# Wider contractions, joined scores and column halves in the attention stages of a three-block fp32 kernel

## The reference

```
# first block: 16 meta tokens are put ahead of the 512; queries see keys up to their own position
h = concatenate([meta, x])
y_sb = stick_breaking(q_sb, k_sb, v_sb)              # 4 heads of 64
y_sp = indexed_sparse_attention(...)                 # 4 heads of 64, top-k keys, softmax
p = softmax(q1 k1 + bias) - lam * softmax(q2 k2 + bias);  y_df = p @ v   # 4 heads, values 128 wide
# second block, nsa part: 6 query heads, 2 groups of keys, 3 kinds of keys, gated and added
kc = gelu(blk @ w1[0]) @ w2[0]; vc = gelu(blk @ w1[1]) @ w2[1]   # 31 compressed keys, blk 2048 wide, w1 2048x256
o = g0 * softmax(q kc) vc + g1 * softmax(q ks) vs + g2 * softmax(q kw) vw
# second block, rwkv part: 4 heads, a state of 64x64 each, carried over 512 tokens
state = state * w_t + sa * (kk_t * a_t) + v_t * k_t;  out_t = state @ r_t
# second block, moba part: 6 heads, causal softmax attention
```

## Time and profile before

| | |
|---|---|
| median of 3 runs | 2671.15 us |
| the profiled execution, its own time | 2670.03 us |
| its span | 2668.2 us |
| TensorE busy | 2564.4 us, 96% |
| VectorE, ScalarE, GpSimd busy | 56%, 39%, 11% |
| granted TensorE clock, mean | 0.985 |

### The profile page before, as it was taken

The page is one execution under the profiler, slowest core; times in us unless marked ns, Lnnn a source line. Parts: engine busy times, 40 slices in busy tenths (PEclk is TensorE's granted clock), DMA queues, the critical chain, the costliest instruction groups (busy, mean ns, idle before and its releaser), DMA issues.

```text
span 2668.2 us, 36243 instructions
## 1 busy us (share of the span) xinstructions
PE 2564.4 (96%) x14684; PEld 2083.5 (78%) x14684; DVE 1481.2 (56%) x2439; ACT 1028.3 (39%) x1817; POOL 300.0 (11%) x213
## 2 busy tenths in 40 slices
PE   8899999999999999999989999999999999999998
PEld 6688898999998877866567777878866687788886
DVE  4887644554445457476546877454744634433544
ACT  4465454443223253235543223254333333322323
POOL 0053210012222010000012222020000000000001
PEclk9999999999999999999999999999999999999999
DMA  4211122222323341520025664332221123233332
GB/s 170 84 53 56 50 63 64 72 87 88 95 89 94 95 143 48 173 72 2 1 95 169 196 203 142 95 103 88 87 71 56 56 87 95 79 95 95 95 95 71
DMA packets 76979, 244.81 MB, mean 92 GB/s; under 512 B 12708, under 2 KB 18213, under 8 KB 76558
## 3 DMA queue, kind: packets, MB, share of 16 engines
q1 hardware_dynamic: 69470, 215.72, 26.3%
q10 hardware_dynamic: 7344, 26.77, 3.0%
HBM read 238.25 MB, written 6.90 MB: 92 GB/s over the span
## 4 chain that ended last, share of the span: by engine, by line
PE 65%; DVE 10%; ACT 4%; issue 2%; POOL 0%; DMA 0%; SPq 0%; ACTq 0%; DVEq 0%
PE ps L595 54%; DVE wl L379 2%; PE ps L2766 2%; ACT wh L367 1%; DVE arena L1064 1%; PE ps L3453 1%; PE ps L1795 1%; PE ps L1824 1%; DVE xl L676 1%; PE ps L1813 1%; DVE arena L3123 1%; PE ps L769 1%; PE ps L3437 1%; PE ps L1660 1%; PE ps L1545 0%
## 5 line engine op out<-in xcount | busy, mean ns | idle before, releaser
L595 PE MATMUL ps<-xh,wh 128*128 128x512 f32 (+1 forms) x2728 | 1007.3, 384 | 22.7 <-DVE xl L676 7.4
L595 PE MATMUL ps<-xl,wh 128*128 128x512 f32 (+1 forms) x2728 | 989.3, 377 | 0.0
L595 PE MATMUL ps<-xh,wl 128*128 128x512 f32 (+1 forms) x2728 | 985.2, 376 | 0.0
L379 DVE TENSOR_TENSOR wl<-ring,wh 128x1024 fp32r<-128x1024 f32 x374 | 472.3, 1263 | 595.4 <-ACT wh L367 594.6
L367 ACT ACTIVATE wh<-ring 128x1024 fp32r<-128x1024 f32 x372 | 393.1, 1057 | 943.0 <-PE ps L595 841.4
L595 PEld LDWEIGHTS ps<-xh,wh 128*128 128x128 f32 x2728 | 500.9, 189 | 149.6 <-issue 40.6
L595 PEld LDWEIGHTS ps<-xh,wl 128*128 128x128 f32 x2728 | 500.4, 189 | 98.0
L595 PEld LDWEIGHTS ps<-xl,wh 128*128 128x128 f32 x2728 | 499.1, 189 | 97.3 <-issue 5.5
L2046 PE MATMUL ps<-xh,wh 128*128 128x264 f32 (+1 forms) x816 | 254.5, 312 | 5.3 <-DVE xl L433 3.8
L759 POOL TENSOR_TENSOR arena<-arena 128x512 f32<-128x512 f32 (+1 forms) x35 | 60.2, 1725 | 1637.0 <-ACT arena L744 1637.0
L2046 PE MATMUL ps<-xl,wh 128*128 128x264 f32 (+1 forms) x816 | 233.4, 286 | 0.0
(11 more groups left out here) (387 smaller groups left out, 2583.2 us busy)
## 6 DMA issues: line engine op xcount, KB each, us to landing
ring<-in_weights SPq DMA_DIRECT2D x374, 512.0 KB, 3.6
arena<-in_w_ada ACTq DMA_DIRECT2D x48, 512.0 KB, 4.6
arena<-in_cmp_w SPq DMA_DIRECT2D x2, 2048.0 KB
strip_copies<-strip_scratch SPq DMA_DIRECT2D x8, 327.5 KB, 7.0
arena<-strip_copies SPq DMA_DIRECT2D x8, 264.0 KB, 4.1
out_features<-arena SPq DMA_DIRECT2D x8, 256.0 KB, 2.1
token_scratch<-arena SPq DMA_DIRECT2D x3, 512.0 KB, 6.7
arena<-token_scratch SPq DMA_DIRECT2D x12, 128.0 KB, 4.3
```

The source lines that it names most:

```text
L379: dve.tensor_tensor(flat(self.wl[:, s % 2]), flat(self.ring[:, s % RING]), flat(self.wh[:, s % 2]).bitcast(F32), ALU.subtract).then_inc(se ...
L595: last = pe.matmul(self.place(u, e), w[:, k, :], x[:, k, o:o + m], start=(k == 0 and i == 0), stop=(k == self.chunks - 1 and i == 2))
```

## The change

Six edits; none changes which engine does what, and no DMA is added, removed or moved.

1. `PairAttention`: in steps with more than the meta keys, the transposes of the first 32 keys and the copy take all 128, and line 2603 contracts over all 128 rows of `VM` and `PM` (for the 4-query tile too).
2. `PairCausal`: the compressed shares are transposed, copied and contracted 128 wide in place of 31; the columns beyond the 31 meet rows of `VC` that a new memset has set to zero.
3. `PairCausal`: for the tiles i = 0 and i = 1 the scores of ks and kw come from one matmul of twice as many columns, in the step e = 0; the step e = 1 issues no scores.
4. `RwkvScan`: value part and U part come ahead of the state's part.
5. `Compress`: each first-layer matmul becomes two, on 64 output partitions each.
6. `Compress`, VectorE: the memset of `VC`.

```diff
@@ RwkvScan.tensor
-        def output(c):
-            k = c // 2
+        def within(c, F, f):
+            for h, lo, t in heads:
+                rows = pair_rows(c, h)
+                pe.matmul(out(c, lo, t), F[rows, t], chunks[rows, c // 2, t, f], start=(f == 3 and t == 0), stop=False)
+
+        def across(c):
             for t in range(2):
                 for lo in (0, 64):
-                    pe.matmul(out(c, lo, t), STATE[lo:lo + 64, c % 2, t], AR[lo:lo + 64, t, 1, c], start=(t == 0), stop=False)
-            for stop, F, f in ((False, V[:, k], 3), (True, U, 1)):
-                for h, lo, t in heads:
-                    rows = pair_rows(c, h)
-                    last = pe.matmul(out(c, lo, t), F[rows, t], chunks[rows, k, t, f], start=False, stop=stop and t == 1)
+                    last = pe.matmul(out(c, lo, t), STATE[lo:lo + 64, c % 2, t], AR[lo:lo + 64, t, 1, c], start=False, stop=t == 1)
...
-            output(c)
+            within(c, V[:, k], 3)
+            within(c, U, 1)
+            across(c)
@@ Compress
+        yield 16.9
+        self.core.vec.do(dve, dve.memset(self.VC.rearrange("p a b -> p (a b)"), 0.0))
...
-                    last = pe.matmul(self.place(2 * e + c), self.w1[:, l, c * P:(c + 1) * P], self.X[:, l], start=(l == 0), stop=(l == 15))
+                    for lo in (0, 64):
+                        last = pe.matmul(self.place(2 * e + c)[lo:lo + 64], self.w1[:, l, c * P + lo:c * P + lo + 64], self.X[:, l],
+                                         start=(l == 0), stop=(l == 15))
@@ PairCausal.tensor
         def score(s, x):
+            if x.first:
+                return
...
-                last = pe.matmul(ps[:, m, 0:(x.i + 1) * P], x.q[half, x.i * P:(x.i + 1) * P], x.keys[m][half, 0:(x.i + 1) * P],
-                                 start=True, stop=True)
+                keys, out = x.keys[m][half, 0:nk] if not x.joined else x.keys[m][half, :, 0:nk], ps[:, m, 0:nk]
+                if x.joined:
+                    out = ps[:, m, 0:2 * nk].rearrange("p (e n) -> p e n", e=2)
+                last = pe.matmul(out, x.q[half, x.i * P:(x.i + 1) * P], keys, start=True, stop=True)
...
-                    pe.transpose(ps[0:NCMP, self.bank(s), (e + 1) * P:(e + 2) * P], x.cmp[0][e], ident)
+                    pe.transpose(ps[:, self.bank(s), (e + 1) * P:(e + 2) * P], x.cmp[0][e], ident)
...
-                    last = pe.matmul(out[m], x.cmp[1][m], self.PM[0:NCMP, m * P:(m + 1) * P], start=False, stop=False)
+                    last = pe.matmul(out[m], x.cmp[1][m], self.PM[:, m * P:(m + 1) * P], start=False, stop=False)
@@ PairCausal.vector
-                    dve.wait_ge(self.scores.sem, self.scores.at(s + 1))
+                    dve.wait_ge(self.scores.sem, self.scores.at(sum(not a.first for a in self.steps[:s + 1])))
...
-                dve.tensor_tensor_reduce(out=self.X[:, s % 3, m, 0:nk], in0=core.ps[:, m, 0:nk],
+                dve.tensor_tensor_reduce(out=self.X[:, s % 3, m, 0:nk], in0=core.ps[:, m, x.first:x.first + nk],
@@ PairCausal.scalar
-                    ins = act.activation(self.PM[0:NCMP], ps[0:NCMP, self.bank(s), P:3 * P], ACT.Copy)
+                    ins = act.activation(self.PM, ps[:, self.bank(s), P:3 * P], ACT.Copy)
@@ PairAttention.tensor
-                    last = pe.transpose(ps[0:32, 4, P + m * nq:P + (m + 1) * nq], X[:, m, 0:32], ident[0:nq, 0:nq])
+                    w = P if nk > META else 32
+                    last = pe.transpose(ps[0:w, 4, P + m * nq:P + (m + 1) * nq], X[:, m, 0:w], ident[0:nq, 0:nq])
...
-                last = pe.matmul(out[part], x.VM[0:32, x.v, part], self.PM[0:32, m * nq:(m + 1) * nq], start=True, stop=(blocks == 0))
+                last = pe.matmul(out[part], x.VM[:, x.v, part], self.PM[:, m * nq:(m + 1) * nq], start=True, stop=(blocks == 0))
@@ PairAttention.scalar
-                ins = act.activation(self.PM[0:32, 0:x.maps * nq], ps[0:32, 4, P:P + x.maps * nq], ACT.Copy)
+                w = P if nk > META else 32
+                ins = act.activation(self.PM[0:w, 0:x.maps * nq], ps[0:w, 4, P:P + x.maps * nq], ACT.Copy)
```

More of the change, by code:

```diff
@@ L1545, in tensor @@
                     last = pe.matmul(state(lo, t), F[rows, t], G[rows, t], start=(e == 1 and t == 0), stop=(e == 0 and t == 1))
-            if c < n - 1:
-                last.then_inc(self.s_ready.sem, 1)
-            output(c)
+                if e == 0 and c < n - 1:
+                    last.then_inc(self.s_ready.sem, 1)
+            within(c, V[:, k], 3)
+            within(c, U, 1)
+            across(c)
     def vector(self, dve):
@@ L1739, with __init__ @@
 class Causal:
-    def __init__(self, i, at, width, q, keys, values, gates=None, begins=True, ends=True, cmp=None):
+    def __init__(self, i, at, width, q, keys, values, gates=None, begins=True, ends=True, cmp=None, joined=False):
+        self.joined = joined
+        self.first = i * P + P if joined and not begins else 0
         self.i, self.at, self.width, self.q, self.keys, self.values, self.gates = i, at, width, q, keys, values, gates
@@ L1757, in __init__ @@
         self.tiles = [sum(x.ends for x in steps[:s]) for s in range(n + 1)]
-        self.scores, self.weighed, self.out_used = core.take("scores", n), core.take("out_ready", n), core.take("out_used", self.tiles[n])
+        self.scores, self.weighed, self.out_used = core.take("scores", sum(not x.first for x in steps)), core.take("out_ready", n), core.take("out_used", self.tiles[n])
         self.masked, self.exps, self.probs, self.turned, self.kept = (core.take(a, 2 * n) for a in (
@@ L2977, in second_block @@
     X_cmp, bias = core.area(at + 2560, 2, 4, 3, NCMP), core.area(at + 2560 + 24 * NCMP, 4, NCMP)
+    wide_cmp = core.area(at + 2560, 28 * NCMP)
     at += 8 * T
@@ L3023, in second_block @@
             for e, tile in enumerate((NKS, NKW)):
+                joined = i < 2
                 some = [P2[:, tile] if groups[m] == m else KX[:, e] for m in range(2)]
+                if joined:
+                    some = [P2[:, NKS:NKW + 1] if groups[m] == m else KX for m in range(2)]
                 gates = [GT[:, i, (2 * p + m) * 3 + e + 1:(2 * p + m) * 3 + e + 2] for m in range(2)]
-                last = ([X_cmp[:, m, i, p] for m in range(2)], [VC[0:NCMP, groups[m]] for m in range(2)]) if e == 0 else None
-                steps.append(Causal(i, t, widths[i], Q[p], some, [half(e, g) for g in groups], gates, e == 0, e == 1, last))
+                shares = [wide_cmp[:, o:o + P] for o in (((4 * m + i) * 3 + p) * NCMP for m in range(2))]
+                last = (shares, [VC[:, groups[m]] for m in range(2)]) if e == 0 else None
+                steps.append(Causal(i, t, widths[i], Q[p], some, [half(e, g) for g in groups], gates, e == 0, e == 1, last, joined))
                 t += widths[i]
```

1 line of the change is left out of this document (added).

## The result

The changed kernel takes 2660.29 us, median of 11 runs (2654.14 to 2668.45), against 2671.15 (2667.86 to 2683.82, 11 runs): ratio 0.9948, 95% interval 0.9932 to 0.9965. 2660 was predicted. Its profiled execution took 2661.84 us with a span of 2660.0.

A forecast was written before the change was run, and what follows sets the result against it. TensorE, busy 96% of the span, was taken as the bound; terms of 15.4 us saved, 10.3 of it arriving after waits, led from 2670.0 to 2660 us. The range was 2650 to 2668, the likeliest case 2656 to 2665.

The forecast's parts named there:

- Step 1: First block's attention: meta keys on all rows save 7.8 us of TensorE's time; the wider ScalarE copies add nothing.
- more than 3 us: Sign in the first block: TensorE idle between 125 and 500 us rising by this means the share arriving was too high.
- Step 2: Second attention: the compressed shares join the weighing's group, 1.7 us saved; wider transposes cost 0, at most 0.4 us.
- Step 3: Second attention: joined scores save a mean 0.27 us, 6 times, 1.6 us; bounds 1.2 and 2.2 us.
- Step 4: Scan: three group entries per chunk become two in 15 of 16 chunks, 2.2 us saved; between 1.5 and 2.4.
- Step 5: Compressed keys' first layer: 16 half passes in 0.61 us, cycle 1.50 to 1.52, 2.1 us saved; widest bounds.
- The rival in which the halves run one by one: Keys' first layer: column halves don't run side by side, this edit loses 4 us, whole kernel 2666; chance 0.08.
- Step 6: VectorE's memset of 128 columns costs nothing; without cover 0.3 us.
- The attention's half: Second attention: of 5.5 us saved on TensorE, half, 2.7 us, reaches the end because waits are dense.
- the 4 that the prediction named as a sign: Second attention: TensorE idle rising by more than 4 us means the share of the gain was too high.
- The slow stretches: Rival: around remaining waits, each new half-clock stretch costs up to 6.8 us; two give 2680, slower; chance 0.08.
- one of 14% to the good: Rival: all of the saving arrives and the slow stretch near 1195 us goes, 2651 us; chance 0.14.

The follow-up runs named there:

- step 3 alone: The kernel before with only the joined scores of the first two tiles: 2681.16 us median, ratio 1.0025.
- all steps but step 3: The changed kernel with the joined scores taken back: 2656.21 us median, ratio 0.9939.
- step 1 alone: The kernel before with only the first block's meta keys on all rows: 2665.77 us median, ratio 0.9984.
- Steps 2, 3, 4 and 6 together: The kernel before with only the second attention and scan edits (compressed shares, joined scores, value parts first, memset): 2672.85 us median, ratio 0.9994.

## Why the prediction was right

The forecast was 2660 and the median is 2660.3. Its working held in TensorE's time, was a little too generous in what arrives (10.3 us against 9.6 at equal clock, a difference inside the interval of 1.0), and left out the clock's part in the gain of 10.9 us between the medians. It also took the 10.3 from the profiled execution; from the median of the runs it would have been 2661. These differences nearly cancel, so that the hit to 0.3 us is luck, and the right size is not. The stages in the traces, each between the same two projection products (which start at 113.5 and 536.4, at 1049.1 and 1184.9, and at 1134.8 and 1358.8 us in the kernel before); in brackets the number of kernels:

| stage | steps undone | steps done | difference | foreseen |
|---|---|---|---|---|
| first block, 10.2 to 13.7 us of it slow | 422.7 to 424.7 (5) | 417.1 to 418.1 (4) | -5.6 | -5.8 |
| keys' first layer, none slow | 135.8 to 136.0 (4) | 133.5 to 134.4 (5) | -2.0 | -1.8 |
| second attention, 30.7 us slow | 223.8, 224.0 (2) | 222.0, between 217.0 at 17.1 us and 225.7 at 41.0 | -1.9 | -2.7 |

With step 3 alone the last stage takes 224.5 us, also with 30.7 slow. With all steps but step 3 it takes 225.8 with 41.0 slow, where the changed kernel has 225.7.

- **What bounds the kernel** held: taking TensorE's time away shortens every stage, and adding it lengthens the attention by about half of it or somewhat more.
- **Step 1, 7.8 us.** Right in TensorE's time (0.15 per step on halves, the late start gone). At equal clock 4.7 us (1.0) reach the end, in the traces 5.6, where I had 5.8: at most the share is somewhat too high. Idle, where I had 2 us more, rose by 3.6 with step 1 alone and by 2.1 in the changed kernel, so that the sign that the prediction named ("more than 3 us") didn't come there. One reading of it was wrong: the wider copies on ScalarE do cost, 377 ns instead of 357 for 256 columns and 272 instead of 250 for 128, with the same number of columns, 0.7 us for the 32 of them.
- **Step 2, 1.7 us.** Seen in the groups; not run alone. Steps 2, 3, 4 and 6 together less steps 3 and 4 leave -0.7 us for it, with an interval of about 1.7, so what reaches the end isn't known. The prediction gives as the source of 0.37 us for line 1824; those rows show lines 2603 and 2606. Line 1824 with two products does take 0.37 us in the kernel before (1259.24 to 1259.61).
- **Step 3, 1.6 us.** The groups are as computed (0.63 and 1.05 us) and nothing reaches the end: -0.1 (1.0) alone, and taking it out changes -0.6 (1.5). The 1.4 us of waits that it adds, above all for VectorE, take back what it saves. Why VectorE is later isn't shown; that the first masking starts later is one candidate, and no run tells it apart.
- **Step 4, 2.2 us.** 1.8 (1.0) arrives, more than the half I gave the attention.
- **Step 5, 2.1 us.** Group 0.61 and cycle 1.51 as computed, 2.4 (1.0) at the end, 2.0 in the stage. The rival in which the halves run one by one is excluded by the 0.61.
- **Step 6, nothing.** No run alone.
- **The attention's half.** Steps 2 to 4 together give 1.2 us at equal clock (1.0), 2.7 was the term. It is the term of the sum that may be mis-sized, and step 3, for which it counted 0.8 us, can be more than half of that. The stage's traces give 1.9, and idle rose by 2.5 us (19.6 to 22.1), less than the 4 that the prediction named as a sign.
- **The slow stretches** were a rival of 8% to the bad side and part of one of 14% to the good. They belonged into the forecast itself: they moved in every kernel, also where nothing near them was changed. The means of all runs, 2674.1 and 2660.5 us, differ by 13.6; 9.6 of it is there at equal clock, and 0.0018 of mean clock gives the other 4.0. In the changed kernel's own profile the stretch of 1195 had moved to 1214 and grown to 17.1 us:

```profile
1200.00:1214.20 14.20, 12.92 (x190) 8.71 (x188) 9.76 (x43) 9.06 (x31) 0.00 (x0) 1.00 0.01 2
1214.20:1231.30 17.10, 16.75 (x141) 11.42 (x138) 7.66 (x29) 5.83 (x19) 0.00 (x0) 0.50 0.01 2
```

TensorE is busy for 12.9 of 14.2 us, and then it runs at half clock while 98% busy. No wait over 0.8 us stands ahead of it in these 14.2 us, as one did in the earlier trace rows, so my reading of those rows (a wait, then a slow stretch) isn't the whole rule.

## What to carry to other kernels

Read the distance to the next start, not the duration, and look for groups whose part of the array differs from their neighbours': each such group costs 0.24 us here, 0.15 inside it and 0.09 before it, and merging, widening or lengthening groups takes that away. Before filling a wait or mourning a slow stretch behind it, look who is late at its end: where the next work waits for another engine anyway, TensorE's speed there is free. And when one kernel's runs fall in two heaps, compare at equal clock and as heaps; a part that seems to lose 10 us in the median (step 3) can be one that does nothing at equal clock, and a part that saves 2.4 us there (step 5) can differ by 6.6 in the mean of all runs, 2667.6 against 2674.1.

## What the runs showed of the hardware

- The changes of width cost about the same at three places: 0.15 us at the entry of a group on 128 x 64 (0.59 us in place of 0.74 when two become one), 0.14 where the scan's parts on 32 x 64 and 64 x 64 have one entry fewer (1.17 in place of 1.31), 0.14 where two groups of 16 half passes become one (1.08 in place of 1.22); and 0.09 to 0.10 by which the product ahead takes longer.
- Half passes of 62 columns on the two column halves take 0.029 us each (32 in 1.08 us with 0.15 of entry), full passes 0.10: two halves cost 0.058, 0.6 of a full pass. The Trainium skill ("TensorEngine Tiling (Array Packing)", Instruction Overhead) advises against taking a factor from so short a product; the trace gives 1.7.
- The time at 0.50 after a wait isn't bound to the wait's length: at the same 4.2 us of idle it was 3.4 us in the changed kernel, from 497.4 us just behind the wait, and 6.8 us in the kernel before, from 498.8 us within it; 27.3 us behind 0.93 and 1.64, and 17.1 behind no wait over 0.8 us in the 14.2 us ahead. It goes on while TensorE is 97% busy. What ends it isn't shown.
